# Output projections as three products of rounded halves, in both blocks of a two-block transformer kernel

## The chip, the cores and the metric

One core of a Trainium2 chip runs the whole kernel. The metric is the device time of one execution in microseconds (us); less is better. Three runs of the kernel before gave 1954.74, 1950.62 and 1954.39 us (median 1954.39).

## What is computed

Two blocks, one after the other, on 256 tokens of width 1024, all in float32. Block 1 has two layers: three attention mixers side by side, an output projection `w_o`, a layer norm, a mixture of 16 experts, and a second layer norm. Block 2 puts 16 meta tokens in front (272 rows) and has two layers: an output projection after the mixers, a root-mean-square norm, and a feed-forward part of width 4096. Layer 0 of block 2 mixes a gated delta rule (4 heads) with windowed attention (8 heads); layer 1 is dense attention with 8 heads.

```python
mix = jnp.concatenate([y_mla, y_diff, y_sb], axis=-1) @ w_o[i]          # block 1, (256,1024)@(1024,1024)
h = layer_norm(DEEPNORM_ALPHA * h + mix, ln1_g[i], ln1_b[i])
...
return jnp.concatenate([ya, yb.astype(ya.dtype)], axis=-1) @ w_out      # block 2, layer 0
return dense_mixer(q, k, v) @ w_out                                     # block 2, layer 1
...
u = rmsnorm(h, mlp_norm_g[layer])
h = h + jnp.square(jax.nn.relu(u @ w_ff1[layer])) @ w_ff2[layer]
```

The change touches the four products with `w_o` (two layers) and `w_out` (two layers).

## The kernel before

Every engine has a program of its own, written out by hand, in one file; engines meet at counting semaphores (`x.wait_ge(sem, n)`, `.then_inc(sem, 1)`). Each engine runs its instructions strictly in the order in which they are written. There is no planner: where a line stands is when it runs.

Weights stream through a ring of six slots of 4096 float32 a partition (2 MB each), loaded by SyncE, each load behind a wait that says its slot is free. `slot(n, KC)` is a slot seen as 8 row groups (k) of 512 columns.

A float32 product can be made in two ways here. The plain way is one `mm` on float32 operands (the trace records each as two MATMULs). The other way splits both operands: a rounded half (type fp32r, written by a ScalarE copy) and the rest (VectorE, operand minus rounded half, also fp32r); then hi·hi + lo·hi + hi·lo is three `mm` (one record each). The feed-forward parts of block 2 already work so: `high_part` (ScalarE) and `low_part` (VectorE) take a unit of 2 row groups by 512 columns (`UNIT`, 1024 values a partition); the rounded half goes to one of four buffers (`ff_hi`, given back by `unit_used`), the rest is written over the unit in its ring slot; `hidden` and `products` use them. `hi_ready` and `lo_ready` count the units.

**Block 1, around w_o** (lines 851 to 891 of PE, `feature_major` of ScalarE, `layer_norm` of VectorE). When the mixers are done, PE transposes the mixed rows `y` in four groups of four; ScalarE copies each group from PSUM to `hT` (line 1394 is the `copy` helper; 718 is `mm`). When all four copies are in, PE makes the plain products, in the order row tile 0 half 0, tile 0 half 1, tile 1 half 0, then the transposes of the normed tile 0 (`normed_tile`, L725), then tile 1 half 1; 8 `mm` of 512 columns each. VectorE meanwhile does the layer norm of tile 0. The slots 0 and 1 (w_o) are refilled with expert weights when `mix_mm` says so, slots 2, 3 and 4 after the later `ple` products.

**Block 2, around w_out** (`project_out`, lines 1054 to 1071). For each of 8 output groups of 128 columns: 8 plain `mm` with 272 (layer 0) or 256 (layer 1) columns; VectorE adds the result to the residual `R`, ScalarE squares it (L1593), PE sums the squares two groups later (`mean_square`), and three filler products (`stay_busy`) follow. Then `inverse_root` (L1598, L1599), `scaled` on VectorE, the halves of `uT`, and the first `hidden` products. ScalarE and VectorE split the first two units of `w_ff1` during output groups 5 to 7, the next two between the halves of `uT`. In layer 0 SyncE starts the loads of slots 2 to 5 at `yT_mm` and that of slot 0 (`w_ff1`) at `wo_mm` 4.

**Ahead of it.** In layer 0 of block 2 a triangular inverse runs by levels (`INVERSE`: for two of the chunks 6 levels of four units): PE products, ScalarE copies `X_`, VectorE masks `BT` and updates `U_`. Before that the windowed attention ends and six groups are transposed (L1183). In layer 1 `attend(1)` has four steps: `score`, softmax, `turn` (transposes, copied to `pTs` by ScalarE), `weigh`, and `outputs`, a ScalarE copy to `uT` that lets the next `weigh` start.

## Time and profile before

| | |
|---|---|
| profiled execution: its own time | 1949.42 us |
| its span (first to last instruction) | 1947.6 us |
| median of three other runs | 1954.39 us |
| PE busy | 1727.3 us, 89% |
| PE weight loads | 1201.4 us, 62% |
| VectorE busy | 796.3 us, 41% |
| ScalarE busy | 482.6 us, 25% |
| mean granted TensorE clock | 0.935 of full |
| DMA queue q1 | 338.28 MB, 47.0% of 16 engines |

Busy shares are means over stages with different limits. The chain that ended last is followed back from the last instruction, at each step to what released it. A duration of a MATMUL in the trace is from its start to its modelled end and overlaps the next one: the pace of a stream is its length divided by its count. The granted clock is 1.00 at 2.4 GHz and 0.50 at 1.2 GHz.

### The profile page before, as it was taken

The numbers are of one execution on the slowest core, as the hardware profiler recorded it, in microseconds if no ns is written. First come the engines' busy times: TensorE is split into PE (matmuls) and PEld (weight loads), VectorE is DVE, ScalarE is ACT, GpSimd is POOL, SyncE is SP. The second block draws the span as 40 slices with busy tenths as digits, with TensorE's granted clock in tenths as the row PEclk, the third lists the DMA queues.
The fourth block names the chain that finished last, engine by engine and source line by source line (L and its number), as shares of the span: only waits on it lengthen the run. The fifth ranks groups of instructions, "written<-read, shape, count | busy, mean of one in ns | idle before, by whom it ended". The sixth has DMA issues, their size and how long they took to land.

```text
span 1947.6 us, 22595 instructions
## 1 busy us (share of the span) xinstructions
PE 1727.3 (89%) x9115; PEld 1201.4 (62%) x9115; DVE 796.3 (41%) x1726; ACT 482.6 (25%) x894; POOL 0.5 (0%) x7
## 2 busy tenths in 40 slices
PE   7958999898895899999879986586899999899998
PEld 6644444343574544434347555586689995469998
DVE  7882411000404331100045455655355553726655
ACT  1142111010214211101022341111144442325443
POOL 0000000000000000000000000000000000000000
PEclk9968999999996899999999867697999999999999
DMA  9061489999706058999962000000434443303541
GB/s 309 1 237 38 171 312 391 396 392 367 252 0 237 9 188 309 392 396 392 385 239 87 1 1 1 0 1 1 173 130 173 173 172 134 125 1 111 192 172 65
DMA packets 153353, 347.03 MB, mean 178 GB/s; under 512 B 8240, under 2 KB 15280, under 8 KB 153280
## 3 DMA queue, kind: packets, MB, share of 16 engines
q1 hardware_dynamic: 145904, 338.28, 47.0%
q10 hardware_dynamic: 7376, 7.74, 1.4%
q8 instruction: 50, 0.82, 0.2%
q14 instruction: 23, 0.19, 0.0%
HBM read 344.96 MB, written 1.05 MB: 178 GB/s over the span
## 4 chain that ended last, share of the span: by engine, by line
PE 75%; DMA 9%; DVE 9%; ACT 3%; issue 2%; SPq 2%; DVEq 0%; ACTq 0%
PE ps L718 72%; DMA ring<-in_w_up 8%; DVE ring L1826 3%; SPq L624 2%; DVE arena L1826 1%; PE ps L1094 1%; PE ps L725 1%; DVE ring L1832 1%; DMA ring<-in_w_in 1%; DVE small L1994 0%; ACT hT L1394 0%; ACT arena L1394 0%; DVE ring L1829 0%; PE ps L811 0%; DVE small L2236 0%
## 5 line engine op out<-in xcount | busy, mean ns | idle before, releaser
L718 PE MATMUL ps<-ring,arena 128*64 128x512 f32 (+6 forms) x1728 | 388.2, 585 | 28.3 <-DMA ring<-in_w_up 17.8
L718 PEld LDWEIGHTS ps<-ring,arena 128*64 128x64 f32 (+2 forms) x1728 | 141.4, 146 | 257.6 <-issue 250.6
L718 PE MATMUL ps<-arena_r,ring_r 128*128 128x272 f32 (+1 forms) x1024 | 291.0, 284 | 0.0
L1394 ACT ACTIVATE arena<-ps 128x512 f32<-128x512 f32 (+7 forms) x179 | 79.9, 475 | 536.9 <-PE ps L718 328.1
L718 PEld LDWEIGHTS ps<-arena_r,ring_r 128*128 128x128 f32 x1024 | 192.5, 188 | 0.0
L718 PE MATMUL ps<-arena_r,ff_hi_r 128*128 128x272 f32 (+1 forms) x992 | 186.2, 285 | 2.8 <-DVE hT L1826 2.8
L718 PE MATMUL ps<-ring,hT 128*128 128x512 f32 (+2 forms) x448 | 180.1, 561 | 8.1 <-DMA ring<-in_w_in 2.6
L718 PE MATMUL ps<-ring 128*128 128x128 f32 (+2 forms) x848 | 133.6, 326 | 37.7 <-DVE ring L1826 30.3
L718 PEld LDWEIGHTS ps<-arena_r,ff_hi_r 128*128 128x128 f32 x992 | 154.8, 189 | 3.2 <-DVE hT L1826 3.2
L718 PE MATMUL ps<-arena_r,y_r 128*128 128x272 f32 (+1 forms) x544 | 149.0, 286 | 6.8 <-issue 3.0
L718 PE MATMUL ps<-arena 128*128 128x512 f32 (+9 forms) x420 | 121.3, 487 | 35.9 <-DVE small L1829 18.0
L718 PEld LDWEIGHTS ps<-ring 128*128 128x128 f32 (+2 forms) x848 | 120.5, 225 | 49.6 <-DVE ring L1826 30.0
L718 PEld LDWEIGHTS ps<-ring,hT 128*128 128x128 f32 x448 | 87.5, 198 | 92.9 <-issue 80.1
L718 PE MATMUL ps<-h_r,y_r 128*128 128x272 f32 (+1 forms) x480 | 136.6, 285 | 0.0
L718 PE MATMUL ps<-h,ring 128*128 128x272 f32 (+1 forms) x512 | 120.3, 393 | 3.1 <-DVE h L1832 1.7
L718 PEld LDWEIGHTS ps<-arena 128*128 128x128 f32 (+4 forms) x420 | 67.6, 233 | 75.6 <-issue 33.6
L718 PEld LDWEIGHTS ps<-h,ring 128*128 128x128 f32 x512 | 98.1, 192 | 23.1 <-issue 2.1
L1832 DVE SCALAR_TENSOR_TENSOR arena<-arena,small,ps 128x512 f32<-128x512 f32 x16 | 12.0, 747 | 243.2 <-PE ps L718 243.2
L718 PEld LDWEIGHTS ps<-arena_r,y_r 128*128 128x128 f32 x544 | 100.5, 189 | 9.2 <-issue 3.4
L718 PEld LDWEIGHTS ps<-h_r,y_r 128*128 128x128 f32 x480 | 90.4, 188 | 0.0
L1826 DVE TENSOR_TENSOR ring_r<-ring,y_r 128x1024 fp32r<-128x1024 f32 x64 | 76.9, 1222 | 27.6 <-ACT y_r L1394 27.0
L1826 DVE TENSOR_TENSOR ring_r<-ring,ff_hi_r 128x1024 fp32r<-128x1024 f32 x64 | 76.9, 1221 | 23.9 <-ACT ff_hi_r L1394 23.9
(282 smaller groups left out, 1860.2 us busy)
## 6 DMA issues: line engine op xcount, KB each, us to landing
ring<-in_w_down SPq DMA_DIRECT2D x32, 2048.0 KB, 14.5
ring<-in_w_gate SPq DMA_DIRECT2D x32, 2048.0 KB, 17.5
ring<-in_w_up SPq DMA_DIRECT2D x32, 2048.0 KB, 19.2
ring<-in_w_ff SPq DMA_DIRECT2D x32, 2048.0 KB, 8.6
ring<-in_w_in SPq DMA_DIRECT2D x8, 2048.0 KB, 18.6
ring<-in_w_in_ab SPq DMA_DIRECT2D x5, 2048.0 KB, 12.9
ring<-in_w_o SPq DMA_DIRECT2D x4, 2048.0 KB, 11.7
ring<-in_ple_gate SPq DMA_DIRECT2D x4, 2048.0 KB, 19.8
```

Of the source, the lines that this page charges most:

```text
L624: sp.dma_start(slot(n, k), src).then_inc(slot_full[n], 16)
L718: return pe.matmul(o, lhsT, rhs, start=a, stop=z)
L725: ins = pe.transpose(ps[:, g, j * P:(j + 1) * P], src[:, t, (c0 + j) * P:(c0 + j + 1) * P], ident)
L1094: ins = pe.transpose(ps[0:rows(b), 4 + b, hd * P:hd * P + r], probs[i % 3][0:r, hd, cols(b)], ident[0:r, 0:r])
L1394: return act.activation(o, i, ACT.Copy, scale=scale)
L1826: return dve.tensor_tensor(o, a, b, op)
L1832: return dve.scalar_tensor_tensor(o, a, s, b, op0, op1, accum_out=acc)
```

## The change

All four output projections are made from rounded halves. In block 1 both the transposed rows (`y_high`, `y_low`) and the eight units of `w_o` (`wo_high`, `wo_low`) are split between the transposes and the products; the rounded halves of `w_o` have eight buffers of their own. PE waits for the halves of row tile 0 alone and, in tile 0, for each unit. In block 2 the products run unit by unit (4 output groups at once, in four PSUM banks), not output group by output group. In layer 0 the units 0 to 3 are split during the levels of the inverse, the window heads' values before and in its first level, and those heads' units come first in the products; units 4 to 7 are split as buffers come free. In layer 1 units 0 and 1 are split in step 3 of `attend(1)`, ahead of `outputs(2)`. The first unit of `w_ff1` is now split after all squares and ahead of `inverse_root`, the next three between the halves of `uT`. Cut to its core (constants of other waits, which only move by the new counts, are left out):

```diff
+        WO_UNITS = 8
+
+        def wo_hi(u):
+            return wo_hi_r[u // 2][:, (u % 2) * UNIT:(u % 2 + 1) * UNIT].rearrange("p (k n) -> p k n", k=2)
+
+        def wo_unit(of, u):
+            half, q = u // 4, u % 4
+            return of[:, half * SLOT_W:(half + 1) * SLOT_W].rearrange("p (k n) -> p k n", k=KC)[:, 2 * q:2 * q + 2, :]
 
...
+
+        yw_hi, yd_hi = (view(a, 4 * LT, of=arena_r, pat="p (k s) -> p k s", k=4) for a in (9456, 0))
+        yc_hi = view(0, KC * S, of=arena_r, pat="p (k s) -> p k s", k=KC)
+        Y_HI = [[yd_hi[:, k, :] for k in range(4)] + [yw_hi[:, k, :] for k in range(4)], [yc_hi[:, k, :] for k in range(KC)]]
+        OUT_Q = [(2, 3, 0, 1), (0, 1, 2, 3)]
+        OUT_BANK = [1, 3, 5, 6, 0, 2, 4, 1]
+        OUT_SLOT = [(0, 1), (4, 5)]
+        early = [early_hi_r[:, a:a + UNIT].rearrange("p (k n) -> p k n", k=2) for a in (0, UNIT)]
+        OUT_HI = [ff_hi + ff_hi, early + ff_hi[2:] + ff_hi]
+        OUT_X = [(1, 1, 4, 4), (15, 15, 16, 16)]
+
+        def out_unit(of, L, u):
+
+            return (of[:, OUT_SLOT[L][u // 4] * SLOT_W:(OUT_SLOT[L][u // 4] + 1) * SLOT_W]
+                    .rearrange("p (k n) -> p k n", k=KC)[:, 2 * OUT_Q[L][u % 4]:2 * OUT_Q[L][u % 4] + 2, :])
 
...
@@ -876,15 +907,26 @@
                 pe.wait_ge(sbo_ev, 2 * (l + 1))
 
                 pe.wait_ge(prm_used, l + 1)
-                to_feature_major(y, l + 1)
-                for t in range(NT):
+                for t in range(NT):
+                    turn_tile(y, t)
+                for t in range(NT):
+                    pe.wait_ge(hT_ev, 4 * (l + 1) + 2 * t + 2)
+                    pe.wait_ge(yT_ev, 4 * l + 2 * t + 2)
                     for half in range(2):
-                        if t == 0:
-                            pe.wait_ge(slot_full[half], fullx(l, half))
-                        elif half == 1:
+                        if t == 1 and half == 1:
                             normed_tile(2 * l, 0)
-                        for k in range(KC):
-                            ins = mm(ps[:, 4 + 2 * half + t, :], hT[:, k, t * P:(t + 1) * P], slot(half, KC)[:, k, :], k == 0, k == KC - 1)
+                        for q in range(4):
+                            u = 4 * half + q
+                            if t == 0:
+                                pe.wait_ge(lo_ready, WO_UNITS * l + u + 1)
+                            hi, lo = wo_hi(u), wo_unit(ring_r, u)
+                            for e in range(2):
+                                o, k, c = ps[:, 4 + 2 * half + t, :], 2 * q + e, slice(t * P, (t + 1) * P)
+                                mm(o, yT_lo[:, k, c], hi[:, e, :], k == 0, False)
+                                ins = mm(o, yT_hi[:, k, c], hi[:, e, :], False, False)
+                                if t == 1 and e == 1:
+                                    ins.then_inc(unit_used, 1)
+                                ins = mm(o, yT_hi[:, k, c], lo[:, e, :], False, k == KC - 1)
                         ins.then_inc(mix_mm, 1)
                 stay_busy(2, 3)
                 normed_tile(2 * l, 1)
...
 
-            def project_out(L, full_of, slots):
+            def project_out(L):
 
...
-                    w = slot(slots[half], KC)[:, :, (c % 4) * P:(c % 4 + 1) * P]
-                    for k in range(KC):
-                        ins = mm(ps[:, c % 7, 0:n], w[:, k, :], uT[:, k, 0:n], k == 0, k == KC - 1)
-                    ins.then_inc(wo_mm, 1)
-                    if c >= 2:
-                        mean_square(2 * L + 1, c - 2)
-                mean_square(2 * L + 1, KC - 2)
-                mean_square(2 * L + 1, KC - 1)
+                for u in range(8):
+                    q = OUT_Q[L][u % 4]
+                    if u < 4:
+                        pe.wait_ge(uT_ev, OUT_X[L][u])
+                    pe.wait_ge(lo_ready, OUT_UNITS[L] + u + 1)
+                    hi, lo = OUT_HI[L][u], out_unit(ring_r, L, u)
+                    for j in range(4):
+                        c = 4 * (u // 4) + j
+                        if c == 7 and u == 4:
+                            pe.wait_ge(res_ev, KC * L + 1)
+                        o, w = ps[:, OUT_BANK[c], 0:n], slice(j * P, (j + 1) * P)
+                        for e in range(2):
+                            k = 2 * q + e
+                            mm(o, hi[:, e, w], Y_HI[L][k][:, 0:n], u % 4 == 0 and e == 0, False)
+                            ins = mm(o, hi[:, e, w], uT_lo[:, k, 0:n], False, False)
+                            if j == 3 and e == 1:
+                                ins.then_inc(unit_used, 1)
+                            ins = mm(o, lo[:, e, w], Y_HI[L][k][:, 0:n], False, u % 4 == 3 and e == 1)
+                        if u % 4 == 3:
+                            ins.then_inc(wo_mm, 1)
+                    if u >= 4:
+                        mean_square(2 * L + 1, u - 4)
+                for c in range(4, KC):
+                    mean_square(2 * L + 1, c)
...
 
-                feature_major(l + 1)
+                def y_high(g):
+                    t, c0 = g // 2, 4 * (g % 2)
+                    act.wait_ge(hT_mm, 4 * (1, 4)[l] + g + 1)
+                    copy(yT_hi[:, c0:c0 + 4, t * P:(t + 1) * P], heads(ps[:, g, :])).then_inc(hT_ev, 1)
+
+                def wo_high(u):
+                    if u % 4 == 0:
+                        act.wait_ge(slot_full[u // 4], fullx(l, u // 4))
+                    copy(wo_hi(u), wo_unit(ring, u)).then_inc(hi_ready, 1)
+
+                for t in range(NT):
+                    y_high(2 * t)
+                    y_high(2 * t + 1)
+                    wo_high(2 * t)
+                    wo_high(2 * t + 1)
+                for u in range(4, WO_UNITS):
+                    wo_high(u)
 
...
+                    if which == 1:
+                        act.wait_ge(o_ev, base + i + 1)
+                        copy(yc_hi[:, c:c + n, cols(t)], uT[:, c:c + n, cols(t)]).then_inc(uT_hi_ev, 1)
 
...
+
+            def out_high(L, u):
+                if u % 4 == 0:
+                    act.wait_ge(slot_full[OUT_SLOT[L][u // 4]], OUT_FULL[L][u // 4])
+                act.wait_ge(unit_used, OUT_UNITS[L] + u + 1)
+                copy(OUT_HI[L][u], out_unit(ring, L, u)).then_inc(hi_ready, 1)
 
...
             attend(0, w_prob, w_pT, rows)
+            act.wait_ge(o_ev, ATT_BASE[1])
+            copy(yw_hi, uT[:, A_H:KC, :]).then_inc(uT_hi_ev, 1)
...
+                    if len(chunks) > 1 and lev <= 4:
+                        out_high(0, lev - 1)
...
+                if L == 0:
+                    for t in range(NT2):
+                        act.wait_ge(yT_ev, 4 * DEPTH + t + 1)
+                        copy(yd_hi[:, :, cols(t)], uT[:, 0:A_H, cols(t)]).then_inc(uT_hi_ev, 1)
+                else:
+                    out_high(L, 2)
+                    out_high(L, 3)
+                for u in range(4, 8):
+                    out_high(L, u)
                 for c in range(KC):
                     act.wait_ge(res_ev, KC * L + c + 1)
                     squares(2 * L + 1, c)
-                    if 5 <= c < 7:
-                        first_high_part(c - 5)
+                first_high_part(0)
                 inverse_root(2 * L + 1)
                 for c in range(KC):
                     act.wait_ge(uT_full, KC * (2 * L + 1) + c + 1)
                     copy(uT_hi[:, c, 0:n], uT[:, c, 0:n]).then_inc(uT_hi_ev, 1)
-                    if c in (2, 4):
-                        first_high_part(c // 2 + 1)
+                    if c in (1, 3, 5):
+                        first_high_part((c + 1) // 2)
...
+
+                def y_low(g):
+                    t, c0 = g // 2, 4 * (g % 2)
+                    dve.wait_ge(hT_ev, 4 * (l + 1) + g + 1)
+                    tt(yT_lo[:, c0:c0 + 4, t * P:(t + 1) * P], heads(ps[:, g, :]), yT_hi[:, c0:c0 + 4, t * P:(t + 1) * P].bitcast(F32), ALU.subtract).then_inc(yT_ev, 1)
+
+                def wo_low(u):
+                    dve.wait_ge(hi_ready, WO_UNITS * l + u + 1)
+                    tt(wo_unit(ring_r, u), wo_unit(ring, u), wo_hi(u).bitcast(F32), ALU.subtract).then_inc(lo_ready, 1)
+
+                for t in range(NT):
+                    y_low(2 * t)
+                    y_low(2 * t + 1)
+                    wo_low(2 * t)
+                    wo_low(2 * t + 1)
+                for u in range(4, WO_UNITS):
+                    wo_low(u)
 
...
                         tt(BT[u], AT[u], level_mask(lev, d), ALU.mult).then_inc(bt_ready, 1)
+                    if len(chunks) > 1 and lev == 1:
+                        dve.wait_ge(uT_hi_ev, 1)
+                        tt(uT_lo[:, A_H:KC, :], uT[:, A_H:KC, :], yw_hi.bitcast(F32), ALU.subtract).then_inc(uT_ev, 1)
+                    elif len(chunks) > 1 and lev <= 5:
+                        out_low(0, lev - 2)
...
+                for u in range(4 if L == 0 else 2, 7):
+                    out_low(L, u)
                 for c in range(KC):
                     dve.wait_ge(wo_mm, KC * L + c + 1)
-                    tt(R[:, c, 0:N], R[:, c, 0:N], ps[:, c % 7, 0:N], ALU.add).then_inc(res_ev, 1)
-                    if c >= KC - 2:
-                        first_low_part(c - KC + 2)
+                    tt(R[:, c, 0:N], R[:, c, 0:N], ps[:, OUT_BANK[c], 0:N], ALU.add).then_inc(res_ev, 1)
+                    if c == 3:
+                        out_low(L, 7)
+                first_low_part(0)
                 dve.wait_ge(rs_ready, 2 * L + 2)
                 scaled(2 * L + 1, mlp_g[:, L, :], 0)
                 for c in range(KC):
                     if c + 1 < KC:
                         scaled(2 * L + 1, mlp_g[:, L, :], c + 1)
-                    dve.wait_ge(uT_hi_ev, KC * L + c + 1)
+                    dve.wait_ge(uT_hi_ev, (4 + KC) * L + 4 + c + 1)
                     tt(uT_lo[:, c, 0:N], uT[:, c, 0:N], uT_hi[:, c, 0:N].bitcast(F32), ALU.subtract).then_inc(uT_ev, 1)
-                    if c in (3, 5):
+                    if c in (1, 3, 5):
...
-            attend(1, c_prob, rows)
+            def low_of_heads(i):
+                t, g = ATT[1][i]
+                k = slice(4 * g, 4 * g + 4)
+                dve.wait_ge(uT_hi_ev, 4 + KC + i + 1)
+                tt(uT_lo[:, k, cols(t)], uT[:, k, cols(t)], yc_hi[:, k, cols(t)].bitcast(F32), ALU.subtract).then_inc(uT_ev, 1)
+
+            attend(1, c_prob, rows, lambda i: low_of_heads(i - 2) if i >= 2 else None)
+            out_low(1, 0)
+            out_low(1, 1)
+            low_of_heads(2)
+            low_of_heads(3)
             feed_forward(1)
             for half in range(2):
...
```

## Rows read from the trace of the kernel before

**Rows 1.** Part 4 of the page: the chain that ended last, by engine.
```profile
PE 75%; DMA 9%; DVE 9%; ACT 3%; issue 2%; SPq 2%; DVEq 0%; ACTq 0%
```

**Rows 2.** The chain in order of time: start us, length us, what.
```profile
326.02 20.08 DMA ring<-in_w_up
...
1441.69 169.73 PE ps L718 x1344
...
1768.46 158.75 PE ps L718 x1344
```

**Rows 3.** Timeline, block 1 layer 1: start, us, engine line, xcount [idle before].
```profile
655.83 0.60 ACT L1394 ACTIVATE hT<-ps 128x512 f32<-128x512 f32 x1 [1.21 <-PE ps L725]
...
658.39 0.60 ACT L1394 ACTIVATE hT<-ps 128x512 f32<-128x512 f32 x1 [0.26 <-PE ps L725]
...
659.04 20.87 PE L718 MATMUL ps<-ring,hT 128*128 128x512 f32 x48 [0.69 <-ACT hT L1394]
...
673.08 0.69 DVE L1832 SCALAR_TENSOR_TENSOR h<-h,ps 128x512 f32<-128x512 f32 x1 [5.45 <-PE ps L718]
...
675.29 0.81 DVE L1829 TENSOR_SCALAR h<-h,small 128x1024 f32<-128x1024 f32 x1
```

**Rows 4.** Timeline, block 1 layer 0, the same products.
```profile
167.16 22.71 PE L718 MATMUL ps<-ring,hT 128*128 128x512 f32 x48 [0.69 <-ACT hT L1394]
```

**Rows 5.** Busy time by stretches: PE, PEld, DVE, ACT, POOL, clock, DMA share, GB/s.
```profile
170.00:171.00 1.00, 1.00 (x3) 0.48 (x2) 0.00 (x0) 0.00 (x0) 0.00 (x0) 0.54 0.69 148
171.00:172.00 1.00, 1.00 (x3) 0.40 (x3) 0.00 (x0) 0.57 (x1) 0.00 (x0) 1.00 0.17 27
...
1386.00:1389.60 3.60, 1.45 (x12) 1.18 (x12) 2.81 (x12) 0.00 (x0) 0.00 (x0) 0.98 0.00 0
1389.60:1391.40 1.80, 1.74 (x4) 1.38 (x5) 0.03 (x4) 0.00 (x0) 0.00 (x0) 0.50 0.75 183
1391.40:1395.00 3.60, 3.60 (x13) 2.83 (x13) 0.00 (x0) 0.00 (x0) 0.00 (x0) 0.79 1.01 368
1395.00:1416.00 21.00, 21.00 (x93) 17.43 (x92) 2.63 (x6) 2.58 (x6) 0.00 (x0) 1.00 1.04 394
```

**Rows 6.** Instructions grouped by form, feed-forward of block 2 layer 0 (1441 to 1612).
```profile
L1826 DVE TENSOR_TENSOR ring_r<-ring,y_r 128x1024 fp32r<-128x1024 f32 x28 | 33.6, 1222 | 14.3 <-ACT y_r L1394 14.3
...
L1394 ACT ACTIVATE y_r<-ring 128x1024 fp32r<-128x1024 f32 x28 | 28.8, 1054 | 25.7 <-PE ps L718 25.7
```

**Rows 7.** Timeline, an inverse level of block 2 layer 0.
```profile
1270.30 1.29 DVE L1826 TENSOR_TENSOR ring<-ring,ps 128x512 f32<-128x512 f32 x2 [5.61 <-PE ps L718]
...
1278.80 0.60 ACT L1394 ACTIVATE ring<-ps 128x512 f32<-128x512 f32 x1 [9.76 <-PE ps L718]
```

**Rows 8.** Timeline, projection of block 2 layer 0 and what follows.
```profile
1389.66 12.84 PE L718 MATMUL ps<-h,ring 128*128 128x272 f32 x48 [0.73 <-DVE h L1826]
...
1419.34 1.06 ACT L1394 ACTIVATE y_r<-ring 128x1024 fp32r<-128x1024 f32 x1 [3.52 <-DMA ring<-in_w_ff]
...
1424.68 2.74 PE L718 MATMUL ps<-consts 128*128 128x512 f32 x6
...
1425.87 0.92 DVE L1832 SCALAR_TENSOR_TENSOR h<-hT,small,arena 128x272 f32<-128x272 f32 x2 [1.13 <-ACT arena L1599]
...
1428.12 0.39 PE L718 MATMUL ps<-arena_r,y_r 128*128 128x272 f32 x1 [0.70 <-DVE h_r L1826]
```

**Rows 9.** Timeline, end of attention, projection of block 2 layer 1.
```profile
1713.60 1.54 ACT L1394 ACTIVATE y<-ps 128x512 f32<-128x512 f32 x3 [0.86 <-PE ps L1094]
1716.37 0.60 ACT L1394 ACTIVATE h<-ps 128x512 f32<-128x512 f32 x1 [1.23 <-PE ps L718]
1717.11 3.01 PE L718 MATMUL ps<-y,arena 128*128 128x512 f32 x6 [0.78 <-ACT h L1394]
...
1720.80 10.63 PE L718 MATMUL ps<-h,ring 128*128 128x256 f32 x48 [0.69 <-ACT h L1394]
...
1752.35 2.74 PE L718 MATMUL ps<-consts 128*128 128x512 f32 x6
```

More of the change, by code:

```diff
@@ L176, in program @@
         ff_hi_r = nc.alloc_sbuf_tensor_at("ff_hi_r", [P, 2 * UNIT], F32R, offset=arena_at + 4 * FF_HI)
+        wo_hi_r = [nc.alloc_sbuf_tensor_at(f"wo_hi{i}_r", [P, 2 * UNIT], F32R, offset=arena_at + 8 * UNIT * i) for i in range(4)]
+        yT_hi_r = nc.alloc_sbuf_tensor_at("yT_hi_r", [P, KC * S], F32R, offset=arena_at + 4 * 9472)
+        early_hi_r = nc.alloc_sbuf_tensor_at("early_hi_r", [P, 2 * UNIT], F32R, offset=arena_at + 4 * 4672)
         small = sb("small", 770)
@@ L270, in program @@
         gate_t = tiny(NT * NE)
+        yT_hi = yT_hi_r[:, :].rearrange("p (k s) -> p k s", s=S)
+        yT_lo = hT_r[:, 0:KC * S].rearrange("p (k s) -> p k s", s=S)
+        WO_UNITS = 8
[4 more added lines that the diff above has]
+            return of[:, half * SLOT_W:(half + 1) * SLOT_W].rearrange("p (k n) -> p k n", k=KC)[:, 2 * q:2 * q + 2, :]
         posk_i = view(10816, S)
@@ L513, in program @@
         FF_CHUNKS = D_FF // 512
-        FF_UNITS = [8 * FF_CHUNKS * L for L in range(DEPTH)]
+        OUT_UNITS = [WO_UNITS * DEPTH + (8 * FF_CHUNKS + 8) * L for L in range(DEPTH)]
+        FF_UNITS = [n + 8 for n in OUT_UNITS]
+        OUT_FULL = [wo_full, [woc_full[4], woc_full[5]]]
         def ff_steps(eng, step):
@@ L1052, in mean_square @@
                     ins.then_inc(ms_mm, 1)
-            def project_out(L, full_of, slots):
+            def project_out(L):
                 n = FF_N[L]
-                for c in range(KC):
-                    half = c // 4
-                    if c % 4 == 0:
-                        pe.wait_ge(slot_full[slots[half]], full_of[half])
-                    if c == 7:
-                        pe.wait_ge(res_ev, KC * L + 1)
-                    w = slot(slots[half], KC)[:, :, (c % 4) * P:(c % 4 + 1) * P]
-                    for k in range(KC):
-                        ins = mm(ps[:, c % 7, 0:n], w[:, k, :], uT[:, k, 0:n], k == 0, k == KC - 1)
-                    ins.then_inc(wo_mm, 1)
-                    if c >= 2:
-                        mean_square(2 * L + 1, c - 2)
-                mean_square(2 * L + 1, KC - 2)
-                mean_square(2 * L + 1, KC - 1)
+                for u in range(8):
[22 more added lines that the diff above has]
+                    mean_square(2 * L + 1, c)
                 stay_busy(5, 3)
@@ L1274, in _ @@
                 ins.then_inc(yT_mm, 1)
-            pe.wait_ge(yT_ev, NT2)
-            project_out(0, wo_full, (0, 1))
+            project_out(0)
             def feed_forward(L):
@@ L1374, in _ @@
             pe.wait_ge(o_ev, ATT_BASE[1] + len(ATT[1]))
-            project_out(1, [woc_full[4], woc_full[5]], (4, 5))
+            project_out(1)
             feed_forward(1)
@@ L1809, in _ @@
                     copy(cQT[:, 4 * g:4 * g + 4, t * P:(t + 1) * P], heads(ps[:, 4 * t + g, :])).then_inc(qT2_ev, 1)
-            attend(1, c_prob, c_pT, rows)
+            attend(1, c_prob, c_pT, rows, lambda i: (out_high(1, 0), out_high(1, 1)) if i == 3 else None)
             feed_forward(1)
@@ L2367, in level_mask, with out_low @@
                 return C(f"level{lev}_{'fwd' if d == 0 else 'bwd'}").unsqueeze(1).to_broadcast(shape4)
+            def out_low(L, u):
+                dve.wait_ge(hi_ready, OUT_UNITS[L] + u + 1)
+                tt(out_unit(ring_r, L, u), out_unit(ring, L, u), OUT_HI[L][u].bitcast(F32), ALU.subtract).then_inc(lo_ready, 1)
             dve.wait_ge(tok_ev, 6)
@@ L2455, in _, with low_of_delta @@
             dve.tensor_copy(tB[:, 0:1], oacc[:, 0, 0:1]).then_inc(mix2_ready, 1)
+            def low_of_delta(t):
+                dve.wait_ge(uT_hi_ev, 1 + t + 1)
+                tt(uT_lo[:, 0:A_H, cols(t)], uT[:, 0:A_H, cols(t)], yd_hi[:, :, cols(t)].bitcast(F32), ALU.subtract).then_inc(uT_ev, 1)
             for t in range(NT2):
@@ L2458, in _ @@
                 tt(uT[:, 0:A_H, cols(t)], ps[:, 2 * t, 0:A_H * rows(t)].rearrange("p (c s) -> p c s", c=A_H), tzT[:, :, cols(t)], ALU.mult).then_inc(yT_ev, 1)
+                if t > 0:
+                    low_of_delta(t - 1)
+            low_of_delta(NT2 - 1)
             def feed_forward(L):
```

2 lines of the change are left out of this document (1 added, 1 removed).

## The prediction

> **What bounds the kernel now.** I read the chain that ended last first, then the same chain in order of time, then the timelines of the four projections, then the stretches with their granted clock. The chain is three quarters PE [rows 1], so shorter PE work shortens the kernel where PE runs without a break. All four projections are such places: 48 MATMULs without a gap and only a copy's wait ahead of them [rows 3, 4, 8, 9]. One other stretch is bound differently: the expert weights of block 1, where the chain shows 20.08 us of DMA for one slot [rows 2]. What PE gains ahead of that stretch counts only if the loads also start earlier.
>
> **The price of one product.** Plain: 20.87 us for 48 records of 512 columns are 0.435 us a record, so 0.87 us an `mm` [rows 3]. With 256 columns, 48 records take 10.63 us, 0.443 us an `mm` [rows 9]. Halves: the two feed-forward stretches give 169.73/1344 = 0.126 us a record of 272 columns and 158.75/1344 = 0.118 us for 256 [rows 2]. No fp32r product of 512 columns is in the trace. Array time at full clock is 512/2.4 = 213 ns; the rows at 272 and 256 lie 13 and 11 ns above theirs, so at least 0.213; the ratio 0.126 to 113 ns carried to 512 gives 0.238; the slope between the two rows gives 0.25. I take 0.228, nearest to the fixed 13 ns, and keep 0.213 and 0.25. The far bound is the plain record's own pace, 0.435.
>
> The Trainium skill (TensorE: Matmul & The Clock Gate, Back-to-back issue gap) says that a warm product follows the last after N/2.4 + 2.5 ns, 216 ns for 512 columns. The rows at 272 columns (0.126 against 116 ns by the rule) do not agree; by the rule each layer of block 1 would gain 1.2 us more than I say.
>
> **Block 1, layer 1.** Removed: 32 `mm` at 0.87 = 27.8 us. Added: 96 at 0.228 = 21.9 us, 10.95 a row tile. That alone is 5.9 us. But the products now wait for splits. A copy of a group takes 0.60 us, a ScalarE split of a unit 1.05, a VectorE split 1.22, back to back 1.18 [rows 3, 6].
> - ScalarE: group copies 0 and 1 at 655.83 and 656.7, done 657.3; units 0 and 1 done 658.3 and 659.3; groups 2 and 3 done 660.5; units 2 to 7 at 1.0 each, done 666.5.
> - VectorE (idle since before): rests of groups 0 and 1, then unit 0 done 659.6, unit 1 660.8, rests of groups 2 and 3 at about 0.65 each until 662.1, units 2 to 7 done 663.3 to 669.2.
> - PE: one unit of a row tile is six records, 1.37 us. It starts at 659.6 instead of 659.04, does units 0 and 1, waits 1.0 for unit 2, and from there is slower (1.37) than VectorE (1.18) and never waits again. Tile 0 ends at 659.6 + 10.95 + 1.0 = 671.5 against 659.04 + 13.9 = 672.9: 1.4 gained. Tile 1 has no waits: 13.9 - 10.95 = 2.95 gained. Sum 4.35.
> Cover: behind VectorE's splits stands the layer norm of tile 0. Its second add may start at 671.5, splits end at 669.2; the first add and its statistics (1.4 us) fit between. From that second add to the normed tile are 675.29 + 0.81 - 673.08 = 3.0 us [rows 3], and the half of tile 1 that hides it still takes 5.5. Behind ScalarE's splits stand the loads of `p` and the router and a table load, about 3 us after 666.5, first used past 672. I take 4.3; bounds 2 (0.25 us a record) and 5.8 (0.213 and no wait).
>
> **Block 1, layer 0.** The same, but here the clock is low at the start: 22.71 us instead of 20.87 for the same records [rows 4], low until just before 171 [rows 5]. While it is low PE is slower than the splits and waits for none. If the clock rises where it did, tile 0 gains 2.8 and the layer 5.8; if the slightly later start lets it stay low for one more stretch of some 3.4 us, as short as the low one at 1389.6 [rows 5], it loses 1.6 of that: 4.2. I take 4.9, bounds 2.5 and 7.
>
> Both gains must pass the DMA-bound stretch. Slots 0 to 4 are refilled on `mix_mm` and `ple_mm`, which all lie behind the projection, so all those loads start earlier by what PE gained; only slot 5 does not. I count both whole: 9.2 us.
>
> **Block 2, layer 0.** Removed: 64 `mm` of 272. Added: 192 records at 0.126 = 24.2 us. The order puts units of the window heads first, so PE starts behind the transposes at 1388.95, not at 1389.66 when VectorE has finished [rows 8]. The clock is low from 1389.6 for 3.3 us [rows 5] in both kernels: 15 records there instead of 26, 1.7 us lost, as before. The products and three interleaved square sums (0.46 each) end at 1416.0; then five square sums, the last behind the add and the square of group 7, end at 1418.3, against 1424.68 before (where the fillers start [rows 8]): 6.4 us gained. Splits hide: units 0 to 3 fall into the levels, where VectorE idles 5.61 us and ScalarE 9.76 [rows 7] against 1.22 and 1.05 needed; unit 4's buffer is free after unit 0, its rest ready some 2.5 us later, needed 9 us later; delta-head halves (three copies, three rests, under 4 us) hide beside the first two units, 6 us. The copy for the window heads (1088 values, about 1.1 us) falls into ScalarE's wait for transposes: at most 0.3 lost.
> Not all of it arrives. The first split of `w_ff1` now stands ahead of `inverse_root` on ScalarE, and slot 0 lands only at 1419.34 [rows 8], after a DMA stretch that ran full (share 1.04, 394 GB/s [rows 5]): it is the fifth of five 2 MB loads that start with the transposes, so an earlier issue doesn't bring it. So split 1419.3 to 1420.4, then the two root steps, `scaled` at 1421.6 against 1425.87 [rows 8]: 4.3 left. The first hidden units: VectorE needs 2.9 us a unit (two `scaled` at 0.46, two rests at 0.44, a 1.22 split) where PE needs 3.0, another 0.3 lost. And PE now idles between fillers (end 1420.9) and the first hidden product (1423.9): 3 us. Before, a stretch of 3.6 us with 1.45 busy was followed by the low clock [rows 5], about 1.7 us of loss. I weigh that at two thirds: 1.1. Sum 4.3 - 0.3 - 0.3 - 1.1 = 2.6. Bounds: 1 (low clock, splits seen) and 5.5 (the load lands sooner).
>
> **Block 2, layer 1.** The two early unit splits (2.1 us) stand ahead of `outputs(2)`. ScalarE is done with its three copies at 1715.14 [rows 9], the splits end at 1717.2, `outputs(2)` starts there and not at 1716.37, and the last `weigh` and all behind it is 0.85 late. Products: 192 at 0.118 = 22.7 plus eight square sums (0.43 each, the last ones behind group 7): from 1721.65 to 1747.7, against 1752.35 [rows 9]: 4.65 gained, the 0.85 taken in. All ff slots are loaded; the split of `w_ff1` hides beside the last square sum. The hidden units lose 0.3 as above. 4.3; bounds 2.5 and 5.5.
>
> **Sum.** 4.3 + 4.9 + 2.6 + 4.3 = 16.1 us. From the profiled execution (1949.42): 1933.3. That execution was 5 us under the median of the others (1954.39), so the forecast for a median is between 1949.42 - 16.1 and 1954.39 - 16.1 = 1938.3, nearer the latter: 1937.5.
>
> **Rivals.**
> - A, the clock and the supply eat more. Block 2 has many short low-clock stretches, and an earlier start moves all of them against the work; each is worth up to 1.7 us either way. With two against the change, no rise in layer 0's favour, and 0.25 us a record: 16.1 - 3.4 - 0.7 - 4.2 = 8, 1946. For: the low stretches of [rows 5]. Against: they were there before, and a shift brings as many good as bad ones.
> - B, block 1 gives nothing because the expert stretch is bound by DMA: 16.1 - 9.2 = 7, 1947. For: the DMA pieces in the chain [rows 2]. Against: the loads are released by PE events behind the projection.
> - C, slower. An fp32r record of 512 columns runs at the pace of a plain one, 0.435. The projections of block 1 then take 96 x 0.435 = 41.8 instead of 27.8: 14 lost in each layer where 4.6 were gained, in all 28 - 6.9 = 21 slower, 1975. It decides from 0.29 us a record (27.8/96). For: no row of this width. Against: 256 and 272 columns run at one column a cycle, plain ones at four.
> - D, more: every cover holds, slot 0 lands early, clocks fall well: 2 x 5.8 + 5.5 + 5.5 = 22.6, 1931.
>
> **How the numbers follow.** Forecast 0.73 (11 to 20 us), A 0.09, B 0.06, D 0.05, C 0.03, and 0.04 that the sum of small losses lands within 0.2% (3.9 us, about what a measurement of this kernel can tell from no change). Faster takes forecast, A, B and D: 0.93; same 0.04; slower 0.03. The range takes D's end and all but the rest of A and B: 1931 to 1947.
>
> **What would show it.** Right: records of 512 columns with fp32r operands at about 0.23 us pace in both layers of block 1; one PE wait of about 1 us ahead of unit 2, on VectorE's ring writes; `hT` copies unchanged at 0.60. In block 2 layer 0 a ScalarE wait on the DMA of `w_ff` ahead of the root steps, and from the first product to `scaled` about 32.5 us instead of 36.2. In layer 1 the last `weigh` 0.85 later behind its transposes, products to fillers 26 us instead of 31.5. No new wait in the levels of the inverse. Wrong: a pace over 0.29 us in block 1; waits on `lo_ready` in tile 0 past unit 2; a layer norm of tile 0 that ends after tile 1's first half; levels longer by a microsecond each; the expert stretch of block 1 starting no earlier in its DMA.

## The result, and the profile after

The changed kernel takes 1932.97 us (median of four runs, 1930.90 to 1936.38), the kernel before beside it 1952.75 (1950.62 to 1954.74): a ratio of 0.9914, 95% interval 0.9899 to 0.9929. The forecast was 1937.5, range 1931 to 1947. The profiled execution took 1930.90 us, its span is 1929.1 us and its mean granted clock 0.935, the same as before. That is a mean: single stretches still differ in their clock, as the experiments show.

Parts 1 and 4 of the page of the changed kernel: PE is busy 25 us less, the two splitting engines more, and the chain is still three quarters PE [rows 1].

```profile
PE 1702.4 (88%) x9305; PEld 1210.2 (63%) x9307; DVE 843.6 (44%) x1774; ACT 517.1 (27%) x934; POOL 0.5 (0%) x7
...
PE 74%; DMA 10%; DVE 9%; ACT 3%; issue 2%; SPq 2%; DVEq 0%; ACTq 0%
```

Timeline of the changed kernel, block 1 layer 1, from the transposes of the mixed rows to those of the normed tile (start us, us, engine line, form, [idle before <- releaser]):

```profile
646.95 3.68 PE L756 MATMUL ps<-consts,y 128*128 128x128 f32 x16 [0.47 <-ACT y L1445]
...
651.90 0.47 PE L749 MATMUL ps<-wo_hi_r,hT_r 128*128 128x512 f32 x1 [1.28 <-DVE ring_r L1914]
...
655.28 0.50 PE L749 MATMUL ps<-wo_hi_r,hT_r 128*128 128x512 f32 x1 [0.37 <-DVE ring_r L1914]
...
656.07 0.39 PE L749 MATMUL ps<-wo_hi_r,hT_r 128*128 128x512 f32 x1
...
663.84 0.69 DVE L1920 SCALAR_TENSOR_TENSOR h<-h,ps 128x512 f32<-128x512 f32 x1 [1.61 <-PE ps L749]
...
666.06 0.81 DVE L1917 TENSOR_SCALAR h<-h,small 128x1024 f32<-128x1024 f32 x1
...
668.90 0.39 PE L749 MATMUL ps<-ring_r,yT_hi_r 128*128 128x512 f32 x1
669.13 1.03 PE L756 MATMUL ps<-consts,h 128*128 128x128 f32 x8
```

From 656.07 to 668.90 lie 56 records: 0.229 us each. PE waits twice for VectorE's rests, 1.28 us at the start (0.69 of it was there before [rows 3]) and 0.37 ahead of unit 2, and nowhere after. Tile 0's layer norm ends at 666.9 (666.06 + 0.81), 2.3 us before PE wants it.

The chain of the changed kernel in order of time, where it answers to [rows 2], with one level of the inverse:

```profile
314.43 3.98 SPq L655
...
318.50 20.07 DMA ring<-in_w_up
...
1251.31 12.63 PE ps L749 x96
...
1427.01 169.75 PE ps L749 x1344
...
1749.91 158.75 PE ps L749 x1344
```

The first of the expert loads in the chain starts 7.5 us earlier (326.02 to 318.50) and lasts as long; the feed-forward loops have their old length and start 14.68 and 18.55 us earlier.

Timeline of the changed kernel, block 2 layer 0 behind the products, to set against [rows 8]:

```profile
1407.40 1.06 ACT L1445 ACTIVATE y_r<-ring 128x1024 fp32r<-128x1024 f32 x1 [3.65 <-DMA ring<-in_w_ff]
...
1409.63 0.91 DVE L1920 SCALAR_TENSOR_TENSOR h<-hT,small,arena 128x272 f32<-128x272 f32 x2
...
1411.88 0.58 PE L749 MATMUL ps<-arena_r,y_r 128*128 128x272 f32 x1 [4.20 <-DVE h_r L1914]
```

and the stretches around it, in the columns of [rows 5]:

```profile
1407.00:1409.50 2.50, 0.68 (x2) 0.00 (x0) 1.01 (x1) 1.86 (x3) 0.00 (x0) 1.00 1.02 405
1409.50:1412.20 2.70, 0.32 (x1) 0.32 (x2) 2.46 (x7) 2.04 (x4) 0.00 (x0) 0.95 0.49 196
1412.20:1416.00 3.80, 3.80 (x20) 3.80 (x20) 3.47 (x6) 1.77 (x4) 0.00 (x0) 0.59 0.02 4
```

ScalarE waits 3.65 us for the `w_ff1` load; PE has nothing to do for 4.20 us, and the granted clock then falls for about three microseconds while PE is already busy with hidden products.

Timeline of the changed kernel, the end of attention in block 2 layer 1, against [rows 9]:

```profile
1700.83 1.99 ACT L1445 ACTIVATE early_hi_r<-ring 128x1024 fp32r<-128x1024 f32 x2
...
1702.72 0.57 ACT L1445 ACTIVATE h<-ps 128x512 f32<-128x512 f32 x1
...
1703.44 3.01 PE L749 MATMUL ps<-y,arena 128*128 128x512 f32 x6 [1.32 <-ACT h L1445]
...
1707.13 0.39 PE L749 MATMUL ps<-arena_r,early_hi_r 128*128 128x256 f32 x1 [0.69 <-ACT h L1445]
```

The last `weigh` waits 1.32 instead of 0.78: it is 0.54 us late.

Distances between the same instructions give the gain of each place, free of what happened ahead of it. The marks in block 1 layer 0 (transposes of y, router product) and block 2 layer 0 (delta transposes), kernel before, then changed kernel:

```profile
162.80 3.67 PE L725 MATMUL ps<-consts,y 128*128 128x128 f32 x16 [0.47 <-ACT y L1394]
...
203.50 3.61 PE L718 MATMUL ps<-hT,arena 128*16 128x256 f32 x16
...
1387.49 1.45 PE L1273 MATMUL ps<-consts,ring 128*128 128x128 f32 x12 [1.75 <-DVE small L2455]
```

```profile
162.22 3.67 PE L756 MATMUL ps<-consts,y 128*128 128x128 f32 x16 [0.47 <-ACT y L1445]
...
196.83 3.61 PE L749 MATMUL ps<-hT,arena 128*16 128x256 f32 x16
...
1375.69 1.44 PE L1325 MATMUL ps<-consts,ring 128*128 128x128 f32 x12 [1.75 <-DVE small L2569]
```


| from, to | before | after | gained | forecast |
|---|---|---|---|---|
| block 1 layer 0: transposes of y to router product | 40.70 | 34.61 | 6.09 | 4.9 |
| block 1 layer 1: the same | 38.85 | 34.61 | 4.24 | 4.3 |
| block 2 layer 0: delta transposes to feed-forward loop | 54.20 | 51.32 | 2.88 | 2.6 |
| block 2 layer 1: first product to loop, less the late weigh | 47.66 | 42.78 + 0.54 | 4.34 | 4.3 |
| sum | | | 17.55 | 16.1 |

The span is 18.5 us shorter. The other 0.95 lies outside the four places: 0.58 ahead of the first (162.80 against 162.22) and 1.06 between the two layers of block 1, less 0.7 lost further on. No edit stands at the first two.

### The profile page after: what moved, and what is told of

It is laid out like the page before. It is cut to its first block, busy times and chain, and to the rows that moved or that the text cites. A ratio compares the mean times of both kernels' runs of the same rounds, so it can differ in the third digit from the quotient of the medians.

```text
span 1929.1 us, 23107 instructions
## 1 busy us (share of the span) xinstructions
PE 1702.4 (88%) x9305; PEld 1210.2 (63%) x9307; DVE 843.6 (44%) x1774; ACT 517.1 (27%) x934; POOL 0.5 (0%) x7
## 4 chain that ended last, share of the span: by engine, by line
PE 74%; DMA 10%; DVE 9%; ACT 3%; issue 2%; SPq 2%; DVEq 0%; ACTq 0%
PE ps L749 70%; DMA ring<-in_w_up 8%; DVE ring L1914 3%; SPq L655 2%; DVE arena L1914 1%; DMA ring<-in_w_ff 1%; PE ps L1146 1%; DVE ring L1920 1%; DMA ring<-in_w_in 1%; PE ps L756 1%; DVE ring_r L1914 0%; DVE small L2082 0%; ACT arena L1445 0%; DVE ring L1917 0%; PE ps L842 0%
## 5 line engine op out<-in xcount | busy, mean ns | idle before, releaser
L749 PE MATMUL ps<-arena_r,ring_r 128*128 128x272 f32 (+1 forms) x1152 | 328.1, 285 | 0.0
L749 PEld LDWEIGHTS ps<-arena_r,ring_r 128*128 128x128 f32 x1152 | 217.3, 189 | 0.0
L749 PE MATMUL ps<-arena_r,ff_hi_r 128*128 128x272 f32 (+1 forms) x1056 | 205.4, 286 | 2.8 <-DVE hT L1914 2.8
L749 PE MATMUL ps<-arena_r,y_r 128*128 128x272 f32 (+1 forms) x592 | 164.0, 288 | 10.3 <-DVE h_r L1914 4.8
L749 PE MATMUL ps<-arena 128*128 128x512 f32 (+8 forms) x418 | 123.5, 497 | 36.4 <-DVE small L1917 18.0
L749 PE MATMUL ps<-h_r,y_r 128*128 128x272 f32 (+1 forms) x528 | 151.1, 286 | 0.0
L749 PE MATMUL ps<-ring,hT 128*128 128x512 f32 (+2 forms) x320 | 120.7, 536 | 7.0 <-DMA ring<-in_w_in 2.9
L749 PEld LDWEIGHTS ps<-ring,hT 128*128 128x128 f32 x320 | 61.9, 195 | 60.4 <-issue 49.0
L1445 ACT ACTIVATE ff_hi_r<-ring 128x1024 fp32r<-128x1024 f32 x72 | 75.7, 1055 | 68.7 <-PE ps L749 68.7
L1445 ACT ACTIVATE y_r<-ring 128x1024 fp32r<-128x1024 f32 x70 | 72.1, 1052 | 58.0 <-PE ps L749 54.3
```

Source lines behind the costliest of these rows:

```text
L749: return pe.matmul(o, lhsT, rhs, start=a, stop=z)
L1445: return act.activation(o, i, ACT.Copy, scale=scale)
```

## The experiments

Numbers 1 to 4 ran on one chip, 5 to 8 on a second, 9 and 10 on a third, each time beside the kernel before. A result is the median time, then the ratio to the kernel before with its 95% interval.

**1 and 2: each block alone.** Beside the whole change.

The first keeps the old `project_out` with its 64 plain `mm` a layer, the second the old products of the mixers; against the change:

```diff
-            def project_out(L):
+            def project_out(L, full_of, slots):
```

```diff
-        WO_UNITS = 8
+        WO_UNITS = 0
...
+                to_feature_major(y, l + 1)
```

> The split products in block 1 alone; block 2 as before. My theory: the gain of block 1 is made in its two projections (6.1 and 4.2 us between the trace of before and of the change, of which some 1.2 us in layer 0 is where the clock happened to rise) and passes the expert stretch whole, so 9 to 11 us faster than the kernel before. Rival B (the expert stretch is bound by DMA and swallows it): within 2 us of the kernel before. If the parts add up, this and the next run together give the 18 us of the whole change.

> The split products in block 2 alone; block 1 as before. My theory: 2.9 us in layer 0 (of 6 us of shorter products the rest is given back to the wait for w_ff1 and to a low clock behind it) and 4.3 us in layer 1, so 6 to 8 us faster than the kernel before. Rival (the early splits in the levels of the inverse cost time there too): under 5 us faster, with levels longer than 14.6 us at the same clock.

Measured: block 1 alone 1939.33 us, 0.9954 (0.9940 to 0.9967); block 2 alone 1940.22 us, 0.9956 (0.9941 to 0.9972), the kernel before 1948.99. The product of the two is 0.9910, the whole change 0.9914: the halves add. What block 1 gains (9.7 us, 9 to 11 expected) does pass the expert stretch; rival B falls. The layers of block 1 alone read 34.61 and 34.62 us again. Block 2 alone comes out 8.8 us faster, above the expected 6 to 8. In its trace its two places give 2.94 and 4.34, 7.3 us, as expected, yet its span is 11.7 under that of before. The surplus lies where no product was changed: 1.85 us in block 1 layer 0 and 3.5 from block 1's second router product to the delta transposes (690.48 against 693.96), both with less time at the low clock, less 1.45 lost between the layers of block 1. The levels of the inverse are no longer than before (13.04 and 14.66 us from one to the next), so its rival falls.

**3: the loads of `w_qkv` behind those of `w_ff1`.**

```diff
-                    for half in range(2):
-                        sp.dma_start(slot(4 + half, KC), cols_of("w_qkv_c", half * 512, 512)).then_inc(slot_full[4 + half], 16)
                     sp.wait_ge(wo_mm, 4)
                     ff_load(L, 0, 0, 0)
                     sp.wait_ge(wo_mm, 8)
                     ff_load(L, 0, 1, 0)
+                    for half in range(2):
+                        sp.dma_start(slot(4 + half, KC), cols_of("w_qkv_c", half * 512, 512)).then_inc(slot_full[4 + half], 16)
```

> The change, with the two w_qkv_c loads of block 2 layer 0 issued behind the loads of slots 0 and 1 and not ahead of them. My theory (the landing of w_ff1 in slot 0 holds up inverse_root, and the idle PE then falls to the low clock): w_ff1 lands some 8 us earlier, ScalarE no longer waits for it (3.65 us in the change), scaled starts 3.5 us earlier, PE idles under 1.5 us and the clock stays at 1.00: 5 us faster than the change, 1.7 of it by the clock. Rival (the split of w_ff1 ahead of inverse_root costs by its own length, not by the landing): at most 1 us. Second rival (w_qkv_c then lands too late for layer 1, or the queue delays the later w_ff loads): no gain, with a new wait in the feed-forward loop.

Measured: 1925.45 us, 0.9890 (0.9862 to 0.9919). Timeline of this kernel, the place of the wait:

```profile
1400.93 4.23 SPq L708 DMA_DIRECT2D ring<-in_w_qkv_c  x2
...
1401.34 1.06 ACT L1445 ACTIVATE y_r<-ring 128x1024 fp32r<-128x1024 f32 x1
...
1402.62 2.74 PE L749 MATMUL ps<-consts 128*128 128x512 f32 x6
...
1403.80 0.92 DVE L1920 SCALAR_TENSOR_TENSOR h<-hT,small,arena 128x272 f32<-128x272 f32 x2
...
1406.06 0.39 PE L749 MATMUL ps<-arena_r,y_r 128*128 128x272 f32 x1 [0.71 <-DVE h_r L1914]
```

The split has no wait, PE idles 0.71 instead of 4.20 us, and the first hidden record lasts 0.39, not 0.58: full clock. Transposes to loop take 46.31 us, 5.0 less than in the change, as expected; the time is some 8 us less, which number 10 takes up. This shows that the `w_ff1` load bounded the place and that the low clock behind it was a consequence.

**4: fillers through the wait.**

```diff
-                stay_busy(5, 3)
+                stay_busy(5, 7 if L == 0 else 3)
```

> The change, with seven filler products instead of three behind the square sums of block 2 layer 0, which keeps PE busy for 3.4 us more while ScalarE waits for w_ff1. My theory: the first hidden products then run at the full clock, 1.7 us faster than the change, the landing of w_ff1 stays where it is and scaled starts no earlier. Rival (the clock falls anyway, or the first hidden units are held by VectorE's splits and not by PE's pace): within 0.4 us of the change in the stretch from the first hidden product to the feed-forward loop.

Measured: 1933.49 us, 0.9917 (0.9895 to 0.9940). Timeline, then stretches, of this kernel:

```profile
1406.90 6.17 PE L749 MATMUL ps<-consts 128*128 128x512 f32 x14
...
1410.16 1.06 ACT L1445 ACTIVATE y_r<-ring 128x1024 fp32r<-128x1024 f32 x1 [4.45 <-DMA ring<-in_w_ff]
...
1414.65 0.39 PE L749 MATMUL ps<-arena_r,y_r 128*128 128x272 f32 x1 [1.58 <-DVE h_r L1914]
```

```profile
1412.00:1414.60 2.60, 1.07 (x3) 0.19 (x1) 2.51 (x6) 1.73 (x4) 0.00 (x0) 1.00 0.33 134
1414.60:1418.00 3.40, 3.35 (x26) 3.35 (x27) 2.92 (x6) 2.02 (x5) 0.00 (x0) 1.00 0.02 5
```

The clock part came as expected: 1.00 throughout, and from the first hidden product to the loop 13.61 us instead of 15.13, 1.5 gained. But transposes to loop fell by 0.70 only (51.32 to 50.62), because the load landed 0.8 us later behind the transposes (32.52 to the split, 31.71 in the change). In the seven other traces with the loads in this order (before, the change twice, numbers 1, 2, 5 and 6) the split starts 31.57 to 31.85 us behind the transposes, so 32.52 lies outside what the others show; what delayed the load stays open.

**5: the copies of `outputs(2)` ahead of the two early splits.**

```diff
-                    if between:
-                        between(i)
                     if i > 0:
                         outputs(i - 1)
+                    if between:
+                        between(i)
```

> One swap on ScalarE in the last value block of block 2's attention: the three copies of outputs(2) stand ahead of the two early splits of units 0 and 1 (2 x 1.05 us). Theory (these two splits make the last weigh late): from weigh(2)'s products to weigh(3)'s the distance falls from 4.25 us back to the 3.7 of the kernel before, the project's first product and all behind it come 0.54 us earlier relative to weigh(2), and units 0 and 1, then split some 1 us later, are still there before the first product of the projection. Rival: the wait only moves; unit 0's rest is late and the projection starts with a wait on it, so that from weigh(2) to the feed-forward loop nothing is won. The total should move by 0.5 us, too little for the times: read it in the trace.

Measured: 1935.73 us, 0.9926 (0.9904 to 0.9948), which says nothing at this size. Timeline of this kernel:

```profile
1704.59 2.93 PE L749 MATMUL ps<-arena 128*128 128x512 f32 x6
...
1708.30 3.00 PE L749 MATMUL ps<-y,arena 128*128 128x512 f32 x6 [0.78 <-ACT h L1445]
...
1709.80 2.36 DVE L1914 TENSOR_TENSOR ring_r<-ring,early_hi_r 128x1024 fp32r<-128x1024 f32 x2 [4.48 <-ACT early_hi_r L1445]
...
1712.08 1.29 DVE L1914 TENSOR_TENSOR h_r<-h,arena_r 128x512 fp32r<-128x512 f32 x2
...
1712.86 0.36 PE L749 MATMUL ps<-arena_r,early_hi_r 128*128 128x256 f32 x1 [1.56 <-DVE h_r L1914]
```

The last `weigh` is back at 3.71 us behind the one before, as the theory says. But VectorE does both unit rests before the rest of the outputs that the first product needs, and PE waits 1.56 us for it: from `weigh` to first product 8.27 us, 7.94 in the change. The rival holds: the wait moved, at a loss of 0.33. The order of the change, with its 0.54, is the better of the two.

**6: units 0 and 1 of `w_o` ahead of the outputs of the mixers.** Their rounded halves get a space of their own under a tensor used later, and VectorE's rests follow the same new order.

```diff
+                wo_high(0)
+                wo_high(1)
...
-                for t in range(NT):
-                    y_high(2 * t)
-                    y_high(2 * t + 1)
-                    wo_high(2 * t)
-                    wo_high(2 * t + 1)
-                for u in range(4, WO_UNITS):
+                y_high(0)
+                y_high(1)
+                for u in range(2, 6):
+                    wo_high(u)
+                y_high(2)
+                y_high(3)
+                for u in range(6, WO_UNITS):
```

> In the mixers of block 1, units 0 and 1 of w_o are split ahead of the attention's outputs (halves in a space of their own, under a tensor that is used only later), and the halves of the second row tile's outputs behind unit 5. Theory (the two PE waits of a layer, 0.9 beyond the copy at the start and 0.5 ahead of unit 2, are waits for splits that could have been made before): the first product starts right behind the rests of groups 0 and 1, about 1.2 us earlier relative to the y transposes, no wait stands ahead of unit 2, and from the y transposes to the router's product each layer takes 1.7 us less: 3.4 us in all, about 1929.5 us beside 1933 for the change. Rival 1: the early splits stand in front of the last evictions of the attention, whose transposes come later by as much as is won: 0. Rival 2: the earlier start meets the low clock in layer 0, which the change passed by luck; 1.7 us there are lost again.

Measured: 1931.79 us, 0.9911 (0.9895 to 0.9926); the change beside it 1933.60. In the place itself the gain is there: 33.04 and 32.49 us for the two layers where the change has 34.61 and 34.61. VectorE has the two rests done at 644.7, in a wait that it had anyway, and the first product starts without a wait on them:

```profile
642.35 2.35 DVE L1919 TENSOR_TENSOR ring_r<-ring,wo_early_r 128x1024 fp32r<-128x1024 f32 x2
...
651.00 0.47 PE L751 MATMUL ps<-wo_early_r,hT_r 128*128 128x512 f32 x1
```

Between the two layers, however, 2.9 us were lost (453.01 against 450.12). The expert stretch is as long as before (165.73 us in both); 1.7 of the loss is one group of 16 products. First the changed kernel, then this one:

```profile
630.96 2.05 PE L749 MATMUL ps<-arena,hT 128*128 128x128 f32 x16 [1.18 <-ACT hT L1445]
```

```profile
629.85 3.78 PE L751 MATMUL ps<-arena,hT 128*128 128x128 f32 x16 [1.17 <-ACT hT L1447]
```

The same 16 records at about half the pace: low clock. Another 1.2 us of it lie at 495 to 503. Of all kernels profiled here the distance between the layers is 450.1 to 450.3 in six (the change twice, numbers 1, 3, 4 and 10) and 452.6 to 453.2 in five (numbers 2 and 5, and 6, 7 and 9, which have early units), with 451.18 before. The early units go with the long case three times of three, but so do two kernels without them, and the kernel before has the slow group too (3.56 us); whether they cause it stays open. In the time 1.8 us arrived where 3.4 were expected, and the intervals of the two kernels overlap.

**7: all three together, and 8: the change itself, beside them.**

> The change with the early units of block 1, the loads of block 2's w_qkv behind the first two of w_ff1, and outputs(2) ahead of the early splits in the last attention. Theory (four separate waits on the path, in different stretches): the gains add, 3.4 + 5 + 0.5 = 9 us less than the change, 1924 us where the change has 1933. Rival: the gain of block 1 is taken by the stretch of expert weights, which waits for the DMA, and only 5.5 us of 9 arrive.

> The changed kernel itself, unchanged, beside the three others on the same chip: 1933 us, 0.9914 of the kernel before, and the same waits as in its first trace. It is the base that the three are compared with.

Measured: all three 1926.57 us, 0.9884 (0.9868 to 0.9901); the change 1933.60, 0.9918 (0.9904 to 0.9931). The two intervals don't meet. Local gains against the change's first trace add to 8.7 us (1.9, 2.1, 5.0 and the loss of 0.33 from number 5); 7.0 arrived in the median, where 9 were expected. In its trace 2.7 us were lost between the layers of block 1. The second trace of the change showed what the first had hidden. The stretch at the start of block 1 layer 0, in the columns of [rows 5], in four traces: before, the change again, the change first, block 2 alone.

```profile
167.16:170.50 3.34, 3.34 (x4) 1.51 (x5) 0.00 (x0) 0.00 (x0) 0.00 (x0) 0.50 0.65 75
```

```profile
167.16:170.50 3.34, 2.69 (x6) 2.15 (x7) 3.34 (x5) 3.34 (x6) 0.00 (x0) 0.50 0.61 70
```

```profile
167.16:170.50 3.34, 2.99 (x12) 2.15 (x12) 3.34 (x5) 3.34 (x6) 0.00 (x0) 1.00 0.69 88
```

```profile
167.16:170.50 3.34, 3.34 (x9) 1.44 (x8) 0.00 (x0) 0.00 (x0) 0.00 (x0) 1.00 0.71 87
```

The low clock there comes and goes with the kernel unchanged (the products start at 167.16 in the first trace of the change, at 167.81 in the second). With it the layer takes 40.70 plain (before) and 35.30 by halves (the change again; 35.41 and 35.42 in numbers 3 and 4), without it 38.85 plain (block 2 alone) and 34.61 by halves. Clock for clock the change gains 5.4 or 4.24 us; the 6.09 of the first trace are a low one before and a high one after.

**9 and 10: early units with the later loads, and the later loads alone, again.** Number 7 without the swap, and number 3 as it was.

> The change with the early units of block 1 and the later loads of w_qkv, but without the swap on ScalarE. Theory (the local gains add in the median, the swap costs 0.3): 0.3 us under the version with all three, and 3.7 us less than the version with the later loads alone, beside it on the same chip; about 1925 where the change has 1933.6. From weigh(2) to the project's first product 7.94 us again, not 8.27. Rival: stretches of low clock between the stages eat what block 1 gains, in most executions and not by chance, so that it equals the version with the later loads alone.

> The change with w_qkv's loads behind the first two of w_ff1, a second time. Theory (5.0 us in block 2 layer 0; the other 3.5 us of the first trace were stretches of low clock that happened to fall away): 1928.6, where the change has 1933.6; from the transposes to the feed-forward loop 46.3 us. Rival: the other 3.5 us belong to it, and it comes at 1925 again.

Measured: number 9 1924.16 us, 0.9879 (0.9862 to 0.9897); number 10 1926.91, 0.9890 (0.9872 to 0.9908). Number 10 takes 46.32 us from transposes to loop: the 5.0 in that place are the edit's. Its span of 1925.0 is 5.1 under that of number 8 (1930.1), where number 3's was 7.9 under. Number 3 has its surplus ahead of the moved loads: from block 1's second router product to the delta transposes it takes 690.56 us, number 10 with the same kernel 694.47, and by the granted clock of 30 us stretches it spent some 7 us less of them at the low clock. Behind the place a little is given back: from the feed-forward loop to the third `weigh` of layer 1 the four kernels with the later loads take 272.66 to 272.71 us, the eight other traces 271.66 to 272.18; in number 10 a short low stretch lies some 10 us later than in number 8. Whether the later loads cause this was not tried. The medians (6.7 under number 8's, on another chip) leave open what the edit is worth in all. Number 9 is the fastest kernel of this study, 9.4 us under number 8, on another chip; from `weigh` to first product it has its 7.94 us again. It is 2.75 us under number 10 where 3.7 were expected; their intervals overlap, so that block 1's gain arrives in the total is likely, not shown.

## Why the prediction was right

- **Price of a product.** 0.228 forecast, 0.229 measured. Rival C (0.435, slower from 0.29) is refuted. The two widths in the trace before bracketed the third (0.213 to 0.25), and 0.228 was a choice within.
- **Block 1, layer 1.** 4.3 against 4.24. The two waits came where they were put: the start 0.6 later than a copy's wait (1.28 against 0.69), then one wait ahead of unit 2. That one was 0.37 beyond the end of unit 1's modelled records, about 0.5 of pace, where 1.0 was forecast. The layer norm and ScalarE's loads stayed covered.
- **Block 1, layer 0.** The term that was off most: 4.9 against 6.09. The step said that the clock would rise where it did, or later; it did not allow for a stretch already at full clock. Number 8 shows the forecast's own case, low in both kernels, at 5.4, between its 4.2 and 5.8. So 0.69 of the 1.19 too much is luck with the clock, and 0.5 is the term's own error.
- **The DMA stretch passes it all.** Right; numbers 1 and 2 show it by times, the chain by its load of unchanged length (20.07 us, 20.08 before) that starts 7.5 us earlier.
- **Block 2, layer 0.** 2.6 against 2.88, and by its parts: the split starts 31.71 us behind the delta transposes (31.85 before: the load is not brought forward); from split to `scaled` 2.23 us (2.3 forecast); `scaled` 4.4 earlier (4.3 forecast), 32.6 us behind the first product (32.5 forecast); then the low clock behind the idle PE takes 1.5, which number 4 gives back (1.1 had been set, two thirds of 1.7). The forecast also had a low clock at the first product; it was high in the trace after, so the products ended 7.9 us earlier instead of 6.4, and the wait for the load swallowed the difference. The two losses of 0.3 did not come: from the first hidden product to the loop the traces at full clock take 13.61 us, 13.57 before. So 2.6 came out right partly because a low clock set 0.4 too small and 0.6 of losses that stayed away cancel. The forecast's own times for the products add to 1416.2, not 1416.0, which changes nothing.
- **Block 2, layer 1.** 4.3 against 4.34, with the late `weigh` at 0.54 instead of 0.85: the pair of splits holds ScalarE for 1.8 us (from the end of the three copies at 1700.93 to 1702.72), not 2.1, since each of these copies starts about 0.1 us before the end recorded for the one ahead. First product to fillers took 26.3 us (26 forecast), and the hidden units lost 0.37 (0.3 forecast).
- **Levels of the inverse.** The products of a level take 12.63 us, in two levels 11.00, before and after. But counted from its first product to that of the next, one level takes 13.4 us instead of 13.03 in all nine traces with both blocks changed; number 2, with the same early splits in block 2, does not show it. So a wait of 0.4 us was overlooked, and its cause stays open.
- **The total.** 16.1 forecast, 17.55 in the four places, 18.5 in the span, 19.8 between the medians. The 4.5 us between 1937.5 and 1932.97 are 1.45 in the four places (1.2 of it block 1 layer 0, 0.69 of that by the clock), 0.95 outside them, and 2.1 in the step from the profiled execution to the median: the forecast stands 4.2 above the profiled execution less the sum, and after the change the median lay 2.1 above the profiled execution.

## What to carry to other kernels

When a product stream gets shorter, look at the load that is due at its end: in block 2 layer 0 only 2.9 of some 8 us came through, and moving two unrelated loads behind it gave 5 more in that place. A split that stands in front of a copy is a matter of order on two engines; changing the order on one of them moved the wait to the other. Read a gain between two fixed instructions in both traces, and read the kernel twice: with the kernel unchanged, the clock shifted a 35 us place by 0.7 to 0.8 us (the change and its repeat, numbers 3 and 10) and a stretch of 690 us by 3.9 (numbers 3 and 10).

## What the runs showed of the hardware

- A record with fp32r operands takes 0.229 us with 512 columns, 0.126 with 272 and 0.118 with 256 at full clock. That is 16, 13 and 11 ns over a column a cycle. At the low clock it is 0.43 us with 512 (168.80 to 169.23 in number 8's trace) and 0.229 with 272 (1412.48 to 1412.71 in the change), only some 3 ns over the time of a column a cycle at 1.2 GHz. The Trainium skill (TensorE: Matmul & The Clock Gate, Back-to-back issue gap) gives 216 ns for 512 columns as the gap of an isolated product, and about 131 ns for a sustained stream. The rows agree with neither; by them each layer of block 1 gained 1.2 us less than by the first figure.
- Behind 4.20 us without a product the granted clock fell to a mean of 0.59 over the next 3.8 us although PE was then busy throughout; with 14 filler records in place of 6 the gap was 1.58 us and the clock stayed at 1.00. All twelve traces divide so: behind a gap of 4.0 to 4.2 us (the change twice, numbers 2, 5 and 6) the first hidden product stands 15.1 us ahead of the loop, behind one of 0.7 to 1.6 us (the other seven) 13.6.
- The same stretch of the same kernel ran at 0.50 in one execution and 1.00 in another (167 to 170.5 us): six products of 512 columns were begun in it at the low clock, twelve at the full one.
